# Token-major projections: the gates, branch and output projections of a hybrid block with the weights as the streamed operand

## The chip, the cores and the metric

The kernel is one program on one NeuronCore of one Trainium2 chip. The metric is the device time in microseconds (us) from the first to the last instruction of an execution. The kernel before has a median of 2720.31 us over three runs (2718.95 to 2721.55).

## The reference, cut to what matters

256 tokens of width 2048 pass a mixer (retention and RWKV-7 branches, gated and merged), then an expert layer with 16384 experts. The change touches the second half of the mixer: the two gate projections, the two branch projections, their gated sum, the output projection and the residual.

```python
z = h @ w_in[layer]                       # the last 2*2048 columns of z are the gates
q, k, v, g_ret_out, z_rwkv, gate_ret, gate_rwkv = _split(z, [...])
...
merged = (jax.nn.sigmoid(gate_ret) * (o_ret @ w_ret_branch[layer])
          + jax.nn.sigmoid(gate_rwkv) * (o_rwkv @ w_rwkv_branch[layer]))
x = x + merged @ w_out[layer]
h2 = rms_norm(x, norm2_w[layer])
x = x + peer(h2, ...)
return rms_norm(x, final_norm_w)
```

## The kernel before, in words

Every float32 product is made of three float32r products: both operands are split into a rounded part and a remainder (hi, lo), and hi*hi, hi*lo and lo*hi are added up in PSUM.

**Units and halves.** Weights come in units of 128 partitions x 1024 columns (512 KB). SyncE loads a unit into one of four slots of `raw` (`load_seg`, L280), ScalarE rounds it into `w_hi` in two halves of 512 columns (`hi`, L712; the instruction is L723), VectorE subtracts to get `w_lo` (`lo`, L1071; L1074), and TensorE uses it. `w_hi` and `w_lo` hold two units, so ScalarE may write half n only when half n-4 has been used (`half_used`), and SyncE may load unit n only when unit n-4 has been split (`unit_split`). In the expert layer's first half GpSimd does the subtraction (L1060); in its second half (`vm`, L685) the split is as in the projections.

**Stages.** `SEG` gives for each projection its first unit, its first output group, the groups, the units in a group and the offset in the operand's chunks. In order: `main_rwkv` (52 units), `main_ret` (64), the recurrent part, `gates` (64), `ret` (16), `rwkv` (16), `out` (32), `wq` (32), then the expert layer with 256 units of `peer_u` and 256 of `peer_v`. The stages `gates` to `out` are the 128 units that the change touches.

**A projection** (`project`, L374) keeps the channels of the result on the partitions: a 128x128 block of the weights is the stationary operand and 256 tokens of `act_hi` or `act_lo` (2048 channels on partitions, 256 tokens) stream. A unit takes 24 matmuls of 256 columns, a group is 256 output channels in two PSUM banks of which half is used. The second half of the expert layer (`vm`, L695 to L697) does it the other way: 128 tokens are stationary and 512 weight columns stream, 12 matmuls a unit.

**Between the units** stands other work of the same stages. In `gates` (`head_between`), TensorE does four small sets of matmuls with block-diagonal ones (L593, L599) and a small projection (L606), VectorE one step of the RWKV head norm in each unit from unit 13 (eight reciprocals first, L1327), ScalarE squares and roots. The evacuation of a group stands after the second unit of the next group: sigmoid on ScalarE for `gates` (L803), a product with the gate on VectorE for `ret` (L1359) and `rwkv` (L1362), where the sum of the branches follows (L1364), a copy on ScalarE for `out` (L797). The last group of `gates`, `ret` and `rwkv` is evacuated when TensorE has done the stage; on VectorE the split of the next stage's operand (L1115) or weights comes behind it.

**The end of `out`.** The result has channels on the partitions, so 32 transposes (L618) bring it to tokens on the partitions, VectorE adds x bank by bank (L1373, eight instructions), ScalarE sums the squares (L769, five instructions), and the second norm and its 32 transposes (L416) stand ahead of `wq`. x is loaded again (L320) with the keys behind all loads of `out`.

**PSUM.** Projections use banks 0 to 3, `head_between` uses banks 4 to 7.

## Time and profile before

| | us |
|---|---|
| median of three runs | 2720.31 |
| the profiled execution, whole | 2721.9 |
| its span, first to last instruction | 2720.0 |
| TensorE busy | 2604.2 (96%) |
| VectorE busy | 1738.1 (64%) |
| ScalarE busy | 1259.8 (46%) |
| GpSimd busy | 815.3 (30%) |
| mean granted TensorE clock | 0.988 |

A row of the timeline gives the start and the length of an instruction or of a merged run of them (xcount); the brackets tell how long the engine idled before it and who released it. PE is TensorE, PEld its weight loads, DVE VectorE, ACT ScalarE, SPq the DMA queue of SyncE. Matmuls are pipelined: the length printed of one is longer than the distance to the next, so rates are read from starts. In the rows of stretches each engine has its busy time and, in brackets, its instructions; PEclk is the granted clock as a share of 2.4 GHz.

### The profile page before, as it was taken

Reading aid. Unit: us, or ns where it says so; the run is one execution under the profiler, and the core shown is the slowest. Engines: PE = TensorE matmul, PEld = TensorE weight load, DVE = VectorE, ACT = ScalarE, POOL = GpSimd, SP = SyncE. Lnnn points to the kernel's source line nnn. Section 1 sums busy time; section 2 is a strip of 40 time slices with the busy share of each in tenths; the row PEclk is TensorE's granted clock in tenths of the full one; section 3 lists DMA queues with packets and bytes.
Section 4 is the critical chain, followed back from the end, with each engine's and each line's share of the span. In section 5 each row is a group of like instructions: output and inputs, shape, how many; then the busy total and the mean of one; then the engine's idle time right before and its main releaser. Section 6 shows DMA issues by size and latency. Waiting matters only on the chain.

```text
span 2720.0 us, 57389 instructions
## 1 busy us (share of the span) xinstructions
PE 2604.2 (96%) x18602; PEld 2453.3 (90%) x18602; DVE 1738.1 (64%) x3107; ACT 1259.8 (46%) x2301; POOL 815.3 (30%) x612
## 2 busy tenths in 40 slices
PE   7989988888999999999999999999999999999998
PEld 7989977888999999999999999999988888888876
DVE  4467964333664564558986688778866666666656
ACT  5446532223444444544445543444445555555545
POOL 0021014333000000038988887777730000000000
PEclk9999989999999999999999999999999999999999
DMA  6655530000565556665555555555555565666664
GB/s 203 184 163 163 172 124 1 1 0 0 150 184 163 175 173 180 176 172 178 178 174 173 169 164 158 158 160 157 157 176 192 193 193 193 193 193 192 193 224 162
DMA packets 334661, 429.17 MB, mean 158 GB/s; under 512 B 26885, under 2 KB 299639, under 8 KB 333175
## 3 DMA queue, kind: packets, MB, share of 16 engines
q1 hardware_dynamic: 334583, 428.12, 51.4%
q8 instruction: 50, 0.82, 0.1%
q14 instruction: 28, 0.23, 0.0%
HBM read 423.82 MB, written 4.19 MB: 157 GB/s over the span
## 4 chain that ended last, share of the span: by engine, by line
PE 60%; issue 26%; POOL 10%; DVE 2%; DMA 1%; ACT 1%; POOLq 0%; SPq 0%; DVEq 0%; ACTq 0%
POOL w_lo L1060 9%; PE PS L370 8%; PE PS L371 8%; PE PS L372 8%; PE PS L695 8%; PE PS L696 8%; PE PS L697 8%; PE PS L659 2%; PE PS L534 1%; PE PS L498 1%; PE PS L532 1%; PE PS L523 1%; DVE w_lo L1074 1%; DMA raw<-in_peer_v 0%; PE PS L546 0%
## 5 line engine op out<-in xcount | busy, mean ns | idle before, releaser
L370 PE MATMUL PS<-act_hi,w_hi 128*128 128x256 f32 x4256 | 1218.1, 286 | 30.6 <-DVE w_lo L1074 16.9
L371 PE MATMUL PS<-act_lo,w_hi 128*128 128x256 f32 x4256 | 1207.8, 284 | 0.0
L372 PE MATMUL PS<-act_hi,w_lo 128*128 128x256 f32 x4256 | 1207.6, 284 | 0.0
L1074 DVE TENSOR_TENSOR w_lo<-raw,w_hi 128x512 fp32r<-128x512 f32 x1064 | 720.5, 702 | 308.2 <-ACT w_hi L723 304.9
L1060 POOL TENSOR_TENSOR w_lo<-raw,w_hi 128x512 fp32r<-128x512 f32 x512 | 669.3, 1340 | 675.6 <-ACT w_hi L918 675.6
L370 PEld LDWEIGHTS PS<-act_hi,w_hi 128*128 128x128 f32 x4256 | 819.8, 193 | 37.1 <-issue 19.5
L723 ACT ACTIVATE w_hi<-raw 128x512 fp32r<-128x512 f32 x1064 | 637.7, 624 | 417.0 <-PE PS L372 412.6
L371 PEld LDWEIGHTS PS<-act_lo,w_hi 128*128 128x128 f32 x4256 | 820.1, 193 | 1.0 <-issue 1.0
L372 PEld LDWEIGHTS PS<-act_hi,w_lo 128*128 128x128 f32 x4256 | 819.8, 193 | 0.0
L695 PE MATMUL PS<-w_hi,act_hi 128*128 128x512 f32 x1024 | 399.8, 390 | 3.8 <-DVE w_lo L1074 3.8
L696 PE MATMUL PS<-w_lo,act_hi 128*128 128x512 f32 x1024 | 399.5, 390 | 0.0
L697 PE MATMUL PS<-w_hi,act_lo 128*128 128x512 f32 x1024 | 399.3, 390 | 0.0
L1463 DVE STREAM_TRANSPOSE raw<-raw 128x512 f32<-128x512 f32 x512 | 332.5, 687 | 76.9 <-DMA raw<-in_peer_u 74.6
L918 ACT ACTIVATE w_hi<-raw 128x512 fp32r<-128x512 f32 x512 | 302.9, 627 | 154.3 <-PE PS L372 139.2
L1554 DVE TENSOR_TENSOR act_lo<-big,act_hi 128x256 fp32r<-128x256 f32 x256 | 108.8, 425 | 264.5 <-ACT act_hi L957 258.1
L957 ACT ACTIVATE act_hi<-big 128x256 fp32r (+1 forms) x256 | 106.8, 417 | 321.1 <-PE PS L697 319.7
L695 PEld LDWEIGHTS PS<-w_hi,act_hi 128*128 128x128 f32 x1024 | 192.9, 188 | 44.7 <-DVE w_lo L1074 3.4
L697 PEld LDWEIGHTS PS<-w_hi,act_lo 128*128 128x128 f32 x1024 | 192.9, 188 | 40.3
L696 PEld LDWEIGHTS PS<-w_lo,act_hi 128*128 128x128 f32 x1024 | 192.9, 188 | 39.9
L1471 DVE TENSOR_TENSOR big<-PS,big 128x512 f32 (+1 forms) x64 | 44.2, 691 | 83.1 <-PE PS L659 83.1
L929 ACT ACTIVATE big<-PS 128x256 f32 (+1 forms) x62 | 23.9, 385 | 136.0 <-PE PS L372 136.0
L1489 DVE TENSOR_SCALAR cst<-PS,extra 128x128 f32<-128x128 f32 x256 | 84.8, 393 | 0.0
(243 smaller groups left out, 1684.4 us busy)
## 6 DMA issues: line engine op xcount, KB each, us to landing
raw<-in_peer_u SPq DMA_DIRECT2D x1024, 128.0 KB, 2.7
raw<-in_peer_v SPq DMA_DIRECT2D x256, 512.0 KB, 4.2
raw<-in_w_in SPq DMA_DIRECT2D x180, 512.0 KB, 3.8
raw<-in_w_out SPq DMA_DIRECT2D x32, 512.0 KB, 3.5
raw<-in_peer_w_q SPq DMA_DIRECT2D x128, 128.0 KB, 3.2
raw<-in_w_ret_branch SPq DMA_DIRECT2D x16, 512.0 KB, 3.5
raw<-in_w_rwkv_branch SPq DMA_DIRECT2D x16, 512.0 KB, 3.5
big<-in_x SPq DMA_DIRECT2D x2, 1024.0 KB, 5.9
```

The lines of the kernel that those rows point to most:

```text
L370: pe.matmul(out, wh, xh, start=start, stop=False)
L371: pe.matmul(out, wh, xl, start=False, stop=False)
L372: return pe.matmul(out, wl, xh, start=False, stop=stop)
L695: pe.matmul(out, ah, w_hi[:, k % 2, cols], start=start, stop=False)
L696: pe.matmul(out, ah, w_lo[:, k % 2, cols], start=False, stop=False)
L697: last = pe.matmul(out, al, w_hi[:, k % 2, cols], start=False, stop=stop)
L723: act.activation(w_hi[:, slot % 2, hh * 512:(hh + 1) * 512], raw[:, slot, hh * 512:(hh + 1) * 512], ACT.Copy).then_inc(S["unit_hi"], 1)
L918: act.activation(w_hi[:, k % 2, hh * 512:(hh + 1) * 512].rearrange("p (c s i) -> p c s i", c=4, s=4), u_part(k, 4 * hh, 4), ACT.Copy).then ...
L1060: pool.tensor_tensor(w_lo[:, k % 2, cols].rearrange("p (c s i) -> p c s i", c=4, s=4), u_part(k, 4 * hh, 4), w_hi[:, k % 2, cols].bitcast( ...
L1074: dve.tensor_tensor(w_lo[:, slot % 2, cols], raw[:, slot, cols], w_hi[:, slot % 2, cols].bitcast(f32), ALU.subtract).then_inc(S["unit_spli ...
L1463: dve.transpose(turned, turned).then_inc(S["uT"], 1)
L1554: dve.tensor_tensor(act_lo[:, k % 2, :], g, act_hi[:, k % 2, :].bitcast(f32), ALU.subtract).then_inc(S["act2_split"], 1)
```

## The change

In `gates`, `ret`, `rwkv` and `out` the roles of the operands are exchanged. 128 tokens of `act_hi` or `act_lo` are stationary and 512 weight columns stream; a unit is now 256 input channels x 512 output channels (two chunks), loaded in pieces of 512 columns, and takes 12 matmuls of 512 columns. A group is 512 output channels for all 256 tokens and fills two whole PSUM banks; `gates` has 8 groups of 8 units, `ret` and `rwkv` 4 of 4, `out` 4 of 8. The units of all stages and their number stay.

The results now have tokens on the partitions (`gated`, `merged`). `out` needs its operand with channels on the partitions, so the sum of the branches is transposed, 8 transposes for each 512 channels (`turn_merged`): after units 7, 11 and 15 of `rwkv` and after unit 2 of `out`, into banks 4 to 7. ScalarE and VectorE split the operand straight out of PSUM (`split_act`), for the four parts at units 9 and 13 of `rwkv` and 0 and 4 of `out`. The sum of the branches for a group stands on VectorE in the third unit of the next group (`merge`), for the last group at the end of the stage.

`out` yields x's layout at once: VectorE adds the group in PSUM to x (`evac_out`), ScalarE sums squares in the second unit of a later group (`square_new`), six instead of five instructions. The 32 transposes, the ScalarE copy and the block of eight additions at the end are gone. x and the keys are loaded earlier, behind the loads of the first group of `out` and ahead of the other 24 units' (`load_again`). Evacuations are two instructions of 512 columns for each group of twice the size. `ret`, `rwkv` and `out` are written out in full where they had loops; in `gates` as many units as before are.

```diff
-SEG = {"main_rwkv": (0, 0, 13, 4, 0), "main_ret": (52, 13, 16, 4, 0), "gates": (116, 29, 16, 4, 0), "ret": (180, 45, 8, 2, 0), "rwkv": (196, 53, 8, 2, 8),
-       "out": (212, 61, 8, 4, 0), "wq": (244, 69, 8, 4, 0)}
...

...
-        operand = {"main_rwkv": Z(58, 74), "ret": Z(0, 16), "rwkv": Z(0, 16), "out": Z(58, 74), "wq": Z(16, 32)}
+        def token_loop(eng, name, body):
+            u0, g0, ng, ku, _ = SEG[name]
+            def pair(t):
+                for j in range(2):
...
+            return name in ("ret", "rwkv") and isinstance(g, int) and g == 0 and kq % 2 == 0
+        gated = [flat(Z(82 + 16 * tt, 98 + 16 * tt)) for tt in range(2)]
+        merged = [flat(Z(58 + 8 * tt, 66 + 8 * tt)) for tt in range(2)]
+        def merged_turned(pc):
+            return PS[:, 4 + 2 * (pc % 2):6 + 2 * (pc % 2), :].rearrange("p t (c n) -> p c t n", c=4)
+        def by_chunk(ap):
+            return ap.rearrange("p c (t n) -> p c t n", t=2)
+        operand = {"main_rwkv": None, "ret": Z(0, 16), "rwkv": Z(0, 16), "wq": None}
...
+                def token_body(t, g, base, j):
+                    if name == "out" and g == 1:
+                        load_again()
+                    for kq in range(ku):
+                        slot = kq % 4
+                        sp.wait_ge(S["unit_split"], (base + kq // 4) * 8 + (2 * slot - 6))
+                        sp.dma_start(raw[:, slot, :].rearrange("p (c n) -> p c n", c=2),
+                                     w[:, 2 * kq:2 * kq + 2, ds(g * 512 + col0, 512)]).then_inc(S[f"raw_in{slot}"], 16)
+                if name in BY_TOKEN:
+                    token_loop(sp, name, token_body)
+                    return
...
+            def load_again():
+                sp.wait_ge(S["merged"], 4)
+                sp.dma_start(flat(Z(90, 106)).rearrange("p (a n) -> p a n", a=2),
+                             a["x"][0].rearrange("(a p) n -> p a n", p=P)).then_inc(S["x_again"], 16)
+                sp.dma_start(flat(Z(48, 49))[:, 0:P], a["peer_keys_1"][0]).then_inc(S["keys_in"], 16)
+                sp.dma_start(flat(Z(48, 49))[:, P:2 * P], a["peer_keys_2"][0]).then_inc(S["keys_in"], 16)
...
-            sp.wait_ge(S["merged"], 8)
-            sp.dma_start(flat(Z(90, 106)).rearrange("p (a n) -> p a n", a=2),
-                         a["x"][0].rearrange("(a p) n -> p a n", p=P)).then_inc(S["x_again"], 16)
-            sp.dma_start(flat(Z(48, 49))[:, 0:P], a["peer_keys_1"][0]).then_inc(S["keys_in"], 16)
-            sp.dma_start(flat(Z(48, 49))[:, P:2 * P], a["peer_keys_2"][0]).then_inc(S["keys_in"], 16)
             load_seg("wq", a["peer_w_q"][0], 0)
...
+            def project_tokens(name, between=None):
+                u0, g0, ng, ku, koff = SEG[name]
+                def body(t, g, base, j):
+                    par = (g0 + j) % 2
+                    if name == "out" and g >= 2:
+                        pe.wait_ge(S["x1_done"], 2 * g - 2)
+                    else:
+                        pe.wait_ge(S["proj_evac"], g + (g0 - 1))
+                    for kq in range(ku):
+                        slot, m = kq % 4, base + kq // 4
+                        if name != "gates" and isinstance(g, int) and g == 0 and kq % 2 == 0:
+                            pe.wait_ge(S["act_split"], 4 * nth_operand[name] + (koff + 2 * kq) // 4 + 1)
+                        for hh in range(2):
+                            kc = koff + 2 * kq + hh
+                            cols = slice(hh * 512, (hh + 1) * 512)
+                            first, last_k = kq == 0 and hh == 0, kq == ku - 1 and hh == 1
+                            pe.wait_ge(S["unit_split"], m * 8 + (2 * slot + hh + 1))
+                            for tt in range(2):
+                                out = PS[:, 2 * par + tt, :]
+                                ah, al = act_hi[:, kc, tt * P:(tt + 1) * P], act_lo[:, kc, tt * P:(tt + 1) * P]
+                                pe.matmul(out, ah, w_hi[:, slot % 2, cols], start=first, stop=False)
+                                pe.matmul(out, ah, w_lo[:, slot % 2, cols], start=False, stop=False)
+                                last = pe.matmul(out, al, w_hi[:, slot % 2, cols], start=False, stop=last_k)
+                            last.then_inc(S["half_used"], 1)
+                        if between and isinstance(g, int):
+                            between(g * ku + kq)
+                token_loop(pe, name, body)
...
                     last.then_inc(S["gate_up"], 1)
-            project("gates", head_between)
-            project("ret")
-            project("rwkv")
-            project("out")
-            pe.wait_ge(S["proj_evac"], 69)
-            for gi in range(8):
-                tt, cg = gi // 4, gi % 4
-                for c in range(4):
-                    last = pe.transpose(PS[:, gi, c * P:(c + 1) * P], big[:, 4 * cg + c, tt * P:(tt + 1) * P], ident)
-                last.then_inc(S["dT_done"], 1)
+            project_tokens("gates", head_between)
+            project_tokens("ret")
+            def turn_merged(pc):
+                pe.wait_ge(S["merged"], pc + 1)
+                if pc >= 2:
+                    pe.wait_ge(S["act_split"], 4 * nth_operand["out"] + pc - 1)
+                for tt in range(2):
+                    for c in range(4):
+                        last = pe.transpose(PS[:, 4 + 2 * (pc % 2) + tt, c * P:(c + 1) * P],
+                                            merged[tt][:, (4 * pc + c) * P:(4 * pc + c + 1) * P], ident)
+                last.then_inc(S["merged_T"], 1)
+            def rwkv_turns(unit):
+                if unit in (7, 11, 15):
+                    turn_merged(unit // 4 - 1)
+            def out_turns(unit):
+                if unit == 2:
+                    turn_merged(3)
+            project_tokens("rwkv", rwkv_turns)
+            project_tokens("out", out_turns)
             pe.wait_ge(S["keys_in"], 32)
             pe.wait_ge(S["x1_done"], 8)
             for w in range(2):
...
+                def body(t, g, base, j):
+                    for kq in range(ku):
...
+                        for hh in range(2):
+                            hi(base + kq // 4, kq % 4, hh)
+                        if kq == 1 and evac and not (isinstance(g, int) and g == 0):
+                            act.wait_ge(S["half_used"], base * 8)
+                            evac(g - 1, (g0 + j + 1) % 2)
+                        if between and isinstance(g, int):
+                            between(g * ku + kq)
+                token_loop(act, name, body)
+                if evac:
+                    act.wait_ge(S["half_used"], 2 * (u0 + ng * ku))
+                    evac(ng - 1, (g0 + ng - 1) % 2)
             def split_act(name, kq):
                 pc = SEG[name][4] // 4 + kq
...
+                    return
                 if name in ("main_rwkv", "wq"):
                     act.wait_ge(S["xT_done" if name == "main_rwkv" else "x2T_done"], pc + 1)
                     for kc in range(4 * pc, 4 * pc + 4):
...
@@ -798,11 +898,11 @@
                                    PS[:, 2 * par:2 * par + 2, 0:TOK], ACT.Copy).then_inc(S["proj_evac"], 1)
                 return evac
-            def evac_sigmoid(base):
-                def evac(g, par):
-                    act.activation(big[:, ds(g * 2 + base, 2), :] if not isinstance(g, int) else big[:, base + 2 * g:base + 2 * g + 2, :],
-                                   PS[:, 2 * par:2 * par + 2, 0:TOK], ACT.Sigmoid).then_inc(S["proj_evac"], 1)
-                return evac
+            def evac_sigmoid(g, par):
+                for tt in range(2):
+                    dst = gated[tt][:, g * 512:(g + 1) * 512] if isinstance(g, int) else gated[tt][:, ds(g * 512, 512)]
+                    last = act.activation(dst, PS[:, 2 * par + tt, :], ACT.Sigmoid)
+                last.then_inc(S["proj_evac"], 1)
             split_seg("main_rwkv", evac_copy(32))
...
@@ -893,14 +993,25 @@
                 if 0 <= q < 2:
...
-            split_seg("gates", evac_sigmoid(82), head_between)
+            split_tokens("gates", evac_sigmoid, head_between)
             sqrt_table()
-            split_seg("ret")
-            split_seg("rwkv")
-            split_seg("out", evac_copy(0))
-            for tt, k, at, end in ((0, 0, 0, 2), (0, 1, 2, 4), (1, 0, 0, 2), (1, 1, 2, 3), (1, 2, 3, 4)):
-                act.wait_ge(S["x1_done"], 4 * tt + end)
-                square(xs[tt][:, 512 * at:512 * end], xn[tt][:, 512 * at:512 * end], tt, k)
+            split_tokens("ret")
+            def rwkv_turned(unit):
+                if unit in (9, 13):
+                    split_act("out", unit // 4 - 2)
+            def out_turned(unit):
+                if unit in (0, 4):
+                    split_act("out", 2 + unit // 4)
+            def square_new(g, par):
+                k, at = max(0, g - 1), 0 if g == 1 else 512 * g
+                for tt in range(2 if g > 0 else 0):
+                    act.wait_ge(S["x1_done"], 2 * g + tt + 1)
+                    square(xs[tt][:, at:512 * g + 512], xn[tt][:, at:512 * g + 512], tt, k)
+            split_tokens("rwkv", None, rwkv_turned)
+            split_tokens("out", square_new, out_turned)
             act.wait_ge(S["kT_done"], 1)
             act.activation(keysT, PS[:, 7, 0:256], ACT.Copy).then_inc(S["keysT"], 1)
             norm(xs, xn, 1)
...
@@ -1348,29 +1484,47 @@
                 for start, steps in stages:
                     if unit >= start:
                         next(steps, None)
...
-            def chunks2(g, base):
-                return big[:, base + 2 * g:base + 2 * g + 2, :] if isinstance(g, int) else big[:, ds(g * 2 + base, 2), :]
             def evac_ret(g, par):
-                dve.tensor_tensor(chunks2(g, 82), PS[:, 2 * par:2 * par + 2, 0:TOK], chunks2(g, 82), ALU.mult).then_inc(S["proj_evac"], 1)
+                for tt in range(2):
+                    cols = gated[tt][:, g * 512:(g + 1) * 512]
+                    last = dve.tensor_tensor(cols, PS[:, 2 * par + tt, :], cols, ALU.mult)
+                last.then_inc(S["proj_evac"], 1)
             def evac_rwkv(g, par):
-                dve.tensor_tensor(chunks2(g, 98), PS[:, 2 * par:2 * par + 2, 0:TOK], chunks2(g, 98), ALU.mult).then_inc(S["proj_evac"], 1)
+                for tt in range(2):
+                    cols = gated[tt][:, 2048 + g * 512:2048 + (g + 1) * 512]
+                    last = dve.tensor_tensor(cols, PS[:, 2 * par + tt, :], cols, ALU.mult)
+                last.then_inc(S["proj_evac"], 1)
...
+            def merge(g):
                 dve.wait_ge(S["proj_evac"], g + (SEG["rwkv"][1] + 1))
-                dve.tensor_tensor(chunks2(g, 58), chunks2(g, 82), chunks2(g, 98), ALU.add).then_inc(S["merged"], 1)
-            dve.wait_ge(S["proj_evac"], 45)
-            split_seg("ret", evac_ret)
-            split_seg("rwkv", evac_rwkv)
-            split_seg("out")
-            dve.wait_ge(S["x_again"], 16)
...
-                dve.wait_ge(S["dT_done"], gi + 1)
-                cols = slice(gi * 512, (gi + 1) * 512)
-                dve.tensor_tensor(flat(Z(90, 106))[:, cols], flat(Z(90, 106))[:, cols], PS[:, gi, :], ALU.add).then_inc(S["x1_done"], 1)
+                for tt in range(2):
+                    last = dve.tensor_tensor(merged[tt][:, g * 512:(g + 1) * 512], gated[tt][:, g * 512:(g + 1) * 512],
+                                             gated[tt][:, 2048 + g * 512:2048 + (g + 1) * 512], ALU.add)
+                last.then_inc(S["merged"], 1)
...
+                    split_act("out", 2 + unit // 4)
+            def evac_out(g, par):
+                if g == 0:
+                    dve.wait_ge(S["x_again"], 16)
+                for tt in range(2):
+                    x1 = flat(Z(90 + 8 * tt, 98 + 8 * tt))[:, g * 512:(g + 1) * 512]
+                    dve.tensor_tensor(x1, x1, PS[:, 2 * par + tt, :], ALU.add).then_inc(S["x1_done"], 1)
```

In ScalarE's and VectorE's `split_act` for `out`, ScalarE waits for `merged_T` and copies `merged_turned(pc)` from PSUM to `act_hi`, and VectorE subtracts it from the same place into `act_lo`. VectorE's `split_tokens` mirrors ScalarE's, with `later(g - 1)` at the third unit of a group and `later(ng - 1)` at the end.

## Rows read from the trace of the kernel before

**Rows 1.** First part of the page: busy time, share, instructions.
```profile
PE 2604.2 (96%) x18602; PEld 2453.3 (90%) x18602; DVE 1738.1 (64%) x3107; ACT 1259.8 (46%) x2301; POOL 815.3 (30%) x612
```
**Rows 2.** Stretches: gates, out, and most of the expert layer's second half.
```profile
681.50:876.50 195.00, 195.00 (x1570) 190.43 (x1568) 115.44 (x154) 92.54 (x146) 0.00 (x0) 1.00 0.60 173
...
981.70:1075.60 93.90, 93.86 (x768) 93.68 (x768) 45.46 (x65) 42.24 (x68) 0.00 (x0) 0.98 0.66 200
...
2003.00:2600.00 597.00, 596.11 (x2640) 493.68 (x2639) 372.95 (x659) 321.53 (x662) 0.23 (x1) 1.00 0.60 192
```
**Rows 3.** Timeline of PE in out, first and last of 28 matmuls.
```profile
1059.72 0.28 PE L371 MATMUL PS<-act_lo,w_hi 128*128 128x256 f32 x1
...
1062.96 0.28 PE L371 MATMUL PS<-act_lo,w_hi 128*128 128x256 f32 x1
```
**Rows 4.** Timeline of PE in the expert layer's second half, first and last of 16.
```profile
2299.65 0.39 PE L696 MATMUL PS<-w_lo,act_hi 128*128 128x512 f32 x1
...
2303.05 0.39 PE L696 MATMUL PS<-w_lo,act_hi 128*128 128x512 f32 x1
```
**Rows 5.** Timeline of DVE in gates, two of the eight reciprocal steps.
```profile
727.84 1.74 DVE L1327 RECIPROCAL big<-big 128x256 f32<-128x256 f32 x1
729.62 1.29 DVE L1074 TENSOR_TENSOR w_lo<-raw,w_hi 128x512 fp32r<-128x512 f32 x2
730.83 1.75 DVE L1327 RECIPROCAL big<-big 128x256 f32<-128x256 f32 x1
```
**Rows 6.** Timelines of ACT, DVE and PE where one stage follows another.
```profile
876.67 0.60 ACT L803 ACTIVATE big<-PS 128x512 f32<-128x512 f32 x1 [5.12 <-PE PS L372]
...
930.66 0.69 DVE L1359 TENSOR_TENSOR big<-PS,big 128x512 f32<-128x512 f32 x1 [3.80 <-PE PS L372]
931.27 1.21 DVE L1115 TENSOR_TENSOR act_lo<-big,act_hi 128x1024 fp32r<-128x1024 f32 x1
...
933.23 0.36 PE L370 MATMUL PS<-act_hi,w_hi 128*128 128x256 f32 x1 [2.61 <-DVE w_lo L1074]
...
979.58 0.69 DVE L1362 TENSOR_TENSOR big<-PS,big 128x512 f32<-128x512 f32 x1
980.30 0.69 DVE L1364 TENSOR_TENSOR big<-big 128x512 f32<-128x512 f32 x1
```
**Rows 7.** Timelines of PE, DVE and ACT from out's last matmul to the norm.
```profile
1075.32 0.28 PE L372 MATMUL PS<-act_hi,w_lo 128*128 128x256 f32 x1
1076.29 3.71 PE L618 MATMUL PS<-cst,big 128*128 128x128 f32 x32 [0.69 <-ACT big L797]
...
1083.16 0.16 DVE L1120 TENSOR_REDUCE small<-small 128x2 f32<-128x6 f32 x1 [1.25 <-ACT big L769]
...
1082.43 0.61 ACT L769 ACTIVATE big<-big 128x512 f32<-128x512 f32 x1
```
**Rows 8.** Stretches around the four changes of stage, for the granted clock (PEclk).
```profile
880.50:887.50 7.00, 5.70 (x27) 5.73 (x28) 4.79 (x7) 3.08 (x6) 0.00 (x0) 0.51 0.46 139
...
930.00:933.00 3.00, 0.63 (x6) 0.42 (x4) 2.34 (x3) 0.63 (x1) 0.00 (x0) 1.00 0.00 0
...
983.00:986.50 3.50, 3.50 (x19) 3.50 (x18) 2.14 (x3) 0.98 (x2) 0.00 (x0) 0.51 0.77 227
...
1082.00:1089.00 7.00, 4.41 (x20) 4.07 (x21) 3.38 (x8) 6.47 (x15) 0.00 (x0) 0.51 0.00 0
```
**Rows 9.** Expert layer, second half: timelines of SP, ACT and PE; last the DMA issues' view.
```profile
2602.59 0.38 SPq L352 DMA_DIRECT2D big<-x_scratch  x1
2603.03 0.46 SPq L354 DMA_DIRECT2D big<-in_final_norm_w  x1
...
2617.32 1.15 ACT L723 ACTIVATE w_hi<-raw 128x512 fp32r<-128x512 f32 x2 [3.71 <-DMA raw<-in_peer_v]
...
2618.73 0.80 PE L695 MATMUL PS<-w_hi,act_hi 128*128 128x512 f32 x1 [2.94 <-DVE w_lo L1074]
...
big<-in_x SPq DMA_DIRECT2D x1, 2048.0 KB, 8.3
```

More of the change, by code:

```diff
@@ L31 @@
 NVEC = VROWS + 16
-SEG = {"main_rwkv": (0, 0, 13, 4, 0), "main_ret": (52, 13, 16, 4, 0), "gates": (116, 29, 16, 4, 0), "ret": (180, 45, 8, 2, 0), "rwkv": (196, 53, 8, 2, 8),
-       "out": (212, 61, 8, 4, 0), "wq": (244, 69, 8, 4, 0)}
+SEG = {"main_rwkv": (0, 0, 13, 4, 0), "main_ret": (52, 13, 16, 4, 0), "gates": (116, 29, 8, 8, 0), "ret": (180, 37, 4, 4, 0), "rwkv": (196, 41, 4, 4, 8),
+       "out": (212, 45, 4, 8, 0), "wq": (244, 45, 8, 4, 0)}
+BY_TOKEN = ("gates", "ret", "rwkv", "out")
 U0, V0 = 276, 532
@@ L43 @@
 LANDED["v"] = LANDED["u"] + 64 * (BLOCKS // 2)
-PEEL = {"main_ret": 8, "gates": 4}
+PEEL = {"main_ret": 8, "gates": 2, "ret": 2, "rwkv": 2, "out": 2}
 PREP_MIX, PREP_LORA_IN, PREP_LORA_W, PREP_DECAY, PREP_EXP, PREP_LORA_A, PREP_A = 3, 12, 14, 16, 20, 21, 23
@@ L761, in split_act @@
                     act.wait_ge(S["orwkv"], 2)
-                if name == "out":
-                    act.wait_ge(S["merged"], 2 * pc + 2)
-                    act.wait_ge(S["half_used"], 2 * SEG["rwkv" if pc < 2 else "out"][0])
                 act.activation(act_hi[:, 4 * pc:4 * pc + 4, :], operand[name][:, 4 * pc:4 * pc + 4, :], ACT.Copy).then_inc(S["act_hi"], 1)
@@ L1083, in body @@
                         ahead = name in ("main_rwkv", "wq") and kq == 0
-                        if name in operand and isinstance(g, int) and g == 0 and not (name == "out" and kq < 2) and not ahead:
+                        if name in operand and isinstance(g, int) and g == 0 and not ahead:
                             split_act(name, kq)
@@ L1095, in split_seg @@
                 seg_loop(dve, name, body, PEEL[name] if between else 1)
-                if name == "rwkv":
-                    split_act("out", 0)
-                    split_act("out", 1)
                 if evac:
@@ L1374, in _ @@
+            split_tokens("ret", evac_ret)
+            split_tokens("rwkv", evac_rwkv, rwkv_turned, merge)
+            split_tokens("out", evac_out, out_turned)
             norm(1, x_tok, xn_tok)
```

49 lines of the change are left out of this document (45 added, 4 removed).

## The prediction, made before the changed kernel was run

> **What bounds the kernel now.** I read the page first: TensorE is busy 96% of the span, VectorE 64%, ScalarE 46% [rows 1]. So time can come only from TensorE's own pace or from the places where it stands still. The view by stretches then shows that this holds in the stages of the change: in `gates` TensorE is busy 195.00 of 195.00 us with 0.60 of the DMA engines' time used, in `out` 93.86 of 93.90 us [rows 2]. A busy share is no pace, so the next view is the timeline of TensorE, read from start to start. In `out` 27 distances take 1062.96 - 1059.72 = 3.24 us, 0.120 us for a matmul of 256 columns [rows 3]. In the expert layer's second half, which already has tokens stationary and 512 weight columns streaming, 15 distances take 2303.05 - 2299.65 = 3.40 us, 0.2267 us for 512 columns [rows 4]. Streaming alone takes 256/2.4 = 107 ns and 512/2.4 = 213 ns at the full clock, so either width carries about 13 ns more for each matmul. A unit costs 24 x 0.120 = 2.88 us now, and 12 x 0.2267 = 2.72 us in the new form. That is the heart of the change. All else is edges: three changes of stage, the end of `out`, and whether the other engines and the loads keep up with 2.72 us.
>
> **The changed stream.** 64 + 16 + 16 + 32 = 128 units x 0.16 us = **-20.5 us**, all on the path. The nearest row is very near: the same shapes, the same split engines, 512 KB for each unit. That stretch holds its pace for 597 us at 192 GB/s with the DMA engines 0.60 used [rows 2], so the loads are no new bound; the pieces of 2 KB (they were 1 KB) lie between the 1 KB of `out`, which ran at 200 GB/s [rows 2], and the 4 KB of the expert layer. Bounds for this term: 0 (the 13 ns are not for each matmul, see the rivals) and -20.5.
>
> **VectorE in `gates`.** The tightest unit holds a reciprocal and two subtractions, 730.83 - 727.84 = 2.99 us from one to the next [rows 5], above 2.72. It happens eight times, units 13 to 20. VectorE may run ahead of TensorE by three halves, 4.08 us, of which rounding and subtracting a half take 0.6 + 0.7 (1.15 and 1.29 for two [rows 5, 9]); 2.7 us are left. A reciprocal in front of a half delays it by 1.75 + 0.65 - 1.36 = 1.05 us, and each unit adds 0.27. TensorE's own insertion after unit 15 (the small projection) gives it time, and the five units behind it reach 1.05 + 4 x 0.27 = 2.1 us. So I take 0, with 2 us as the other bound if that cover fails. ScalarE's crowded place is unit 9, with two sigmoids, two table switches and a root, 4.8 us in a row; behind it stands TensorE's set of matmuls with ones (some 3.4 us), which covers it. Those sets are the same as before.
>
> **The changes of stage.** At the end of `gates` ScalarE evacuates, switches its table and rounds the next operand while TensorE waits: a second sigmoid of 0.60 us stands in this chain now, and the last matmul lasts 0.11 us longer (0.39 for 0.28) [rows 3, 4, 6]: +0.7. At the end of `ret` VectorE evacuates (0.69), splits the operand (1.21) and the first weights, and TensorE stood 2.61 us [rows 6]; a second evacuation goes in: +0.8. At the end of `rwkv` evacuation and sum (0.69 + 0.69, [rows 6]) become four instructions: 2 x 0.69 + 0.11 = +1.5. Queued behind them on VectorE are the first subtraction of `out` and the third part of the operand's split; TensorE is the one who waits. Together **+3.0 us**.
>
> **The transposes.** 32 of them took 3.71 us [rows 7], so 8 take 0.93, and with the late first matmul behind them I take 1.05 for a set (bounds 0.9 and 1.6, the latter if TensorE drains on either side). Four sets: the one after unit 15 of `rwkv` lies in the wait just counted, three are on the path: **+3.2 us**. What each waits for is ready: the sum of group g is done in the third unit of group g+1 and the transposes stand after the fourth. VectorE has in `rwkv` at unit 9 an evacuation (1.38) and a part of the operand's split (1.21), 2.6 us, just under the 2.7 us of its lead, then the sum; I take 0, with 1 us as a bound.
>
> **Sums of squares in `out`.** In unit 17 ScalarE waits for VectorE's additions and then does two squares of 1024 columns, some 3.8 us between two roundings where 4.08 - 0.6 is free: +0.3.
>
> **The end of `out`.** From the start of the last matmul to the reduction that opens the norm now 1083.16 - 1075.32 = 7.84 us pass [rows 7]: a copy, the transposes, eight additions in a row, squares. In the new kernel: 0.43 until the matmul is done, an addition of 0.69, then the second addition beside the first square; the second square starts at about 1.85 and takes 0.61 and a short read of the sum: 2.65 us. **-5.2 us**. What is late next is the same norm and the same 32 transposes as before, with nothing new in front.
>
> **The earlier load of x.** 2 MB and the keys now go out when unit 3 of `out` has been split, ahead of unit 8's weights on SyncE. There is an event like it: 3 MB went out at 2602.59 and 2603.03 amid the streaming of the second half; the next unit's weights were late, ScalarE waited 3.71 us for them until 2617.32 and TensorE stood 2.94 us [rows 9]. So about 11 us of lead were there and 14.7 were needed for 3 MB. 2 MB landed in 8.3 us at the end of `out` [rows 9]; with the unit behind them I get 11 to 12 us. The lead here has one set of transposes more in it, 12 us. I take 0; the other bound is what the 3 MB did, 3 us and a stretch of low clock. VectorE needs x itself only in unit 9, some 16 us after the issue, and is covered.
>
> **The clock.** It fell to half (0.51 where 1.00 is 2.4 GHz) for 7.0 us after the wait at the end of `gates`, for 3.5 us after the one at the end of `rwkv`, not after the 2.61 us at the end of `ret`, and for 7.0 us at the end of `out` [rows 8]. A low stretch costs half its length when TensorE streams. The waits at `ret` and `rwkv` become 0.8 and 1.5 us longer, so a new stretch of 3.5 us is possible at each, 1.7 us of loss; at the end of `out` TensorE now stands still for less. I take +1.0, bounds -2 and +3.5.
>
> **Sum.** -20.5 + 3.0 + 3.2 + 0.3 - 5.2 + 1.0 = -18.2 us. The profiled execution has a span of 2720.0 us in 2721.9; it is 1.6 us above the median of 2720.31. The new span is 2701.8, and against the median 2720.3 - 18.2 = **2702 us**.
>
> **A page beside it.** The Trainium skill, "TensorE: Matmul & The Clock Gate", section "Back-to-back issue gap", gives N/2.4 plus about 2.5 ns for a single matmul at the full clock, 109 ns at 256 columns and 216 ns at 512. The rows show 120 and 227, so the trace doesn't agree; by that rule the new width would bring an estimated 12 x 2.5 ns a unit, 3.8 us in 128 units instead of 20.5, and the time would be 2719, beside the partial form of rival D. The measurement of both widths in this kernel decides for me.
>
> **The rivals.** *A: the forecast*, 0.72.
>
> *B: the load of x starves the stream.* For it: the row of 3.71 us. Against it: a third fewer bytes, and a set of transposes inside the lead. Price 2.94 us and a low stretch of 7 us, half lost: 6.4 us, 2708. Chance 0.16.
>
> *C: VectorE or ScalarE becomes the bound* in the crowded units (13 to 20 of `gates`, 9 of `rwkv`, 17 of `out`). For it: 2.99 against 2.72, and 2.6 of lead 2.7. Price at most 8 x 0.27 + 1 + 1 = 4 us, 2706. Chance 0.06.
>
> *D: the width brings little.* The 13 ns would then be no fixed share of a matmul but of what surrounds it in a projection (operands, evacuations), and a 512-column matmul would take 0.24 there. Then only the edges are left: +3.0 + 3.2 + 0.3 + 1.0 - 5.2 = +2.3, 2722.6. Against it: rows 4. A part of it, say 15 us of the 20.5 lost, gives 2717 and is no change either. Chance 0.04 for the two.
>
> *E, slower: the clock.* If longer waits and transposes between the stages brought TensorE down and it stayed low through a stage instead of 3.5 or 7 us, each unit would lose its streaming time once more, 12 x 0.213 = 2.6 us. From 18.2 / 2.6 = 7 units on it eats the whole gain; 16 units, the whole of `ret`, cost 41 us and give 2743. For it: three of four edges had a low stretch. Against it: none outlasted 7 us [rows 8], and the form itself ran 597 us at 1.00 [rows 2]. Chance 0.02.
>
> **How the numbers follow.** The likeliest is A, 2702. Its own bounds: 2696.5 (no loss to the clock and 2 us back, sets of 0.9 us, less at the end) to 2706 (sets of 1.6, 3.5 us of clock). Reaching to B and C takes the upper end to 2709. D and E stay outside, 0.06, and some of B. A measurement of this kernel can tell about 0.2%, 5.4 us, from no change. Faster: A, B and C, 0.94. No change: D, 0.04. Slower: E, 0.02.
>
> **What would show it.** Starts 0.227 us apart and 2.72 us from unit to unit in all four stages; 1.05 us for each set of transposes; waits of about 6, 3.5 and 3.9 us (the last with a set in it) between the stages; 2.65 us from the last matmul of `out` to the norm's reduction. B would show as a wait of ScalarE for weights of unit 8 or 9 of `out`, C as TensorE waiting for `w_lo` inside a stage, D as 0.24 us from start to start, E in the granted clock of a whole stage. The prediction is wrong if a stage's pace is above 2.75 us a unit.

## The result, and the profile after

The changed kernel takes 2704.25 us (median of 4 runs, 2702.05 to 2706.31) against 2720.93 of the kernel before: a ratio of 0.9942, 95% interval 0.9926 to 0.9958. The forecast was 2702, 18.2 us less than before; 16.7 us less were measured. The interval of the ratio reaches from 11 to 20 us less, so the times alone can't tell 18.2 from 16.7. The profiled execution is the slowest of the four; it has a span of 2704.5 us, 15.5 less than before.

The stretches of the changed kernel, cut at the same events as in [rows 2] (length, then busy time and instructions of PE, PEld, DVE, ACT, POOL, then the granted clock, the DMA engines' share and GB/s); the stages `gates`, `ret`, `rwkv`, `out`, and the way from `out` to `wq`:

```profile
681.90:866.70 184.80, 184.80 (x802) 150.19 (x800) 115.24 (x154) 91.94 (x145) 0.00 (x0) 1.00 0.62 182
872.60:918.60 46.00, 46.00 (x192) 37.75 (x192) 25.49 (x38) 21.39 (x34) 0.00 (x0) 0.94 0.56 183
922.10:969.10 47.00, 47.00 (x208) 38.84 (x209) 31.06 (x46) 21.02 (x32) 0.00 (x0) 0.96 0.56 179
972.70:1062.70 90.00, 89.87 (x392) 73.87 (x392) 48.41 (x71) 41.62 (x69) 0.00 (x0) 0.98 0.65 211
1062.70:1073.20 10.50, 6.64 (x37) 6.21 (x35) 6.83 (x15) 8.89 (x20) 0.00 (x0) 0.67 0.17 41
```

`gates` fell from 195.0 to 184.8 us with the same work of the other engines in it, and TensorE is still busy all the time. `rwkv` gained nothing: it now holds two sets of transposes and a low stretch of the clock. Inside the stream the timeline of TensorE in `out` reads, first and last of 17 matmuls:

```profile
1039.67 0.39 PE L461 MATMUL PS<-w_hi,act_hi 128*128 128x512 f32 x1
...
1043.30 0.39 PE L462 MATMUL PS<-w_lo,act_hi 128*128 128x512 f32 x1
```

16 distances take 3.63 us, 0.2269 each, as in [rows 4]; a unit is 2.72 us. The edges, from the timelines of PE, of DVE and of PE around one set of transposes:

```profile
872.60 0.77 PE L461 MATMUL PS<-w_hi,act_hi 128*128 128x512 f32 x1 [5.66 <-DVE w_lo L1185]
922.08 0.64 PE L461 MATMUL PS<-w_hi,act_hi 128*128 128x512 f32 x1 [3.21 <-DVE w_lo L1185]
972.68 0.47 PE L461 MATMUL PS<-w_hi,act_hi 128*128 128x512 f32 x1 [2.53 <-DVE w_lo L1185]
...
969.32 1.29 DVE L1500 TENSOR_TENSOR big<-PS,big 128x512 f32<-128x512 f32 x2 [4.09 <-PE PS L463]
970.64 1.29 DVE L1506 TENSOR_TENSOR big<-big 128x512 f32<-128x512 f32 x2
...
945.54 1.03 PE L685 MATMUL PS<-cst,big 128*128 128x128 f32 x8
946.33 0.48 PE L461 MATMUL PS<-w_hi,act_hi 128*128 128x512 f32 x1
946.64 0.40 PE L462 MATMUL PS<-w_lo,act_hi 128*128 128x512 f32 x1
```

The doubled evacuation and sum at the end of `rwkv` stand there as two pairs where [rows 6] has two single ones. A set of transposes takes 0.79 us, and the next matmul is 0.08 late: 0.87. At the end of `out` [rows 7] are answered by

```profile
1062.57 0.39 PE L463 MATMUL PS<-w_hi,act_lo 128*128 128x512 f32 x1
...
1062.99 1.28 DVE L1523 TENSOR_TENSOR big<-big,PS 128x512 f32<-128x512 f32 x2 [4.08 <-PE PS L463]
1065.14 0.16 DVE L1256 TENSOR_REDUCE small<-small 128x2 f32<-128x6 f32 x1 [0.87 <-ACT big L869]
```

1065.14 - 1062.57 = 2.57 us from the last matmul to the norm, for 7.84. The low stretches of the clock (PEclk 0.5, that is 1.2 GHz, where 1.00 is 2.4 GHz), to be held against [rows 8]: the ends of `gates`, `ret` and `rwkv`, then one in the expert layer, whose code is the same in both kernels:

```profile
870.90:877.70 6.80, 5.10 (x12) 4.11 (x13) 5.19 (x7) 3.28 (x6) 0.00 (x0) 0.51 0.40 139
922.10:925.50 3.40, 3.40 (x8) 2.63 (x9) 2.77 (x4) 0.55 (x1) 0.00 (x0) 0.52 0.42 153
973.30:976.70 3.40, 3.40 (x10) 2.67 (x9) 2.87 (x4) 0.63 (x1) 0.00 (x0) 0.52 0.43 157
...
1406.80:1410.20 3.40, 3.02 (x14) 3.02 (x15) 3.37 (x5) 1.22 (x2) 3.40 (x4) 0.52 0.15 38
```

**Where the 15.5 us came from.** Read from first and last starts of matmuls: `gates` -10.2, `ret` -2.7, `rwkv` +0.8, `out` -3.7, the three edges +0.6, +0.7 and +1.3, from the last matmul of `out` to the first of `wq` -4.7 (10.61 for 15.26). That makes -17.9. The work ahead of `gates` came out 0.4 longer and the part behind it 1.9 longer (1631.3 us from `wq` on for 1629.4), both without a change in the code. Of the 1.9, 0.9 is a longer wait behind the burst of [rows 9] (3.81 us for 2.94). The low stretch at 1406.8 cost 0.7: from its first matmul to the next pause of TensorE above 1.2 us 68.81 us pass (1407.18 to 1475.99), in the kernel before 68.12 (1424.33 to 1492.45). That is less than half of its 3.4 us. The likely reason, not tested, is that TensorE doesn't set the pace there: GpSimd (POOL) is busy for all of the 3.40 us in that row, TensorE for 3.02.

### The profile page after: what moved, and what is told of

Its sections match the earlier page's. It is cut to its first block, busy times and chain, and to the rows that moved or that the text cites. A ratio compares the mean times of both kernels' runs of the same rounds, so it can differ in the third digit from the quotient of the medians.

```text
span 2704.5 us, 53711 instructions
## 1 busy us (share of the span) xinstructions
PE 2587.5 (96%) x17066; PEld 2374.2 (88%) x17066; DVE 1735.4 (64%) x3107; ACT 1255.1 (46%) x2295; POOL 814.9 (30%) x612
## 4 chain that ended last, share of the span: by engine, by line
PE 61%; issue 25%; POOL 10%; DVE 2%; DMA 1%; ACT 1%; POOLq 0%; SPq 0%; DVEq 0%; ACTq 0%
POOL w_lo L1171 9%; PE PS L407 9%; PE PS L408 9%; PE PS L409 9%; PE PS L774 8%; PE PS L776 8%; PE PS L775 8%; PE PS L738 2%; PE PS L601 1%; PE PS L565 1%; PE PS L599 1%; PE PS L590 1%; DVE w_lo L1185 1%; DMA raw<-in_peer_v 0%; PE PS L613 0%
## 5 line engine op out<-in xcount | busy, mean ns | idle before, releaser
L407 PE MATMUL PS<-act_hi,w_hi 128*128 128x256 f32 x3232 | 925.3, 286 | 20.2 <-POOL w_lo L1171 12.7
L408 PE MATMUL PS<-act_lo,w_hi 128*128 128x256 f32 x3232 | 916.8, 284 | 0.0
L409 PE MATMUL PS<-act_hi,w_lo 128*128 128x256 f32 x3232 | 916.7, 284 | 0.0
L407 PEld LDWEIGHTS PS<-act_hi,w_hi 128*128 128x128 f32 x3232 | 622.4, 193 | 25.5 <-POOL w_lo L1171 12.8
L408 PEld LDWEIGHTS PS<-act_lo,w_hi 128*128 128x128 f32 x3232 | 622.7, 193 | 0.2 <-issue 0.2
L409 PEld LDWEIGHTS PS<-act_hi,w_lo 128*128 128x128 f32 x3232 | 622.4, 193 | 0.0
L774 PE MATMUL PS<-w_hi,act_hi 128*128 128x512 f32 x1024 | 399.6, 390 | 4.7 <-DVE w_lo L1185 4.7
L775 PE MATMUL PS<-w_lo,act_hi 128*128 128x512 f32 x1024 | 399.3, 390 | 0.0
L776 PE MATMUL PS<-w_hi,act_lo 128*128 128x512 f32 x1024 | 399.2, 390 | 0.0
L461 PE MATMUL PS<-w_hi,act_hi 128*128 128x512 f32 x512 | 203.7, 398 | 11.5 <-DVE w_lo L1185 11.4
L462 PE MATMUL PS<-w_lo,act_hi 128*128 128x512 f32 x512 | 201.6, 394 | 0.0
L463 PE MATMUL PS<-w_hi,act_lo 128*128 128x512 f32 x512 | 201.3, 393 | 0.0
```

The source lines that it names most:

```text
L407: pe.matmul(out, wh, xh, start=start, stop=False)
L408: pe.matmul(out, wh, xl, start=False, stop=False)
L409: return pe.matmul(out, wl, xh, start=False, stop=stop)
L461: pe.matmul(out, ah, w_hi[:, slot % 2, cols], start=first, stop=False)
L774: pe.matmul(out, ah, w_hi[:, k % 2, cols], start=start, stop=False)
L775: pe.matmul(out, ah, w_lo[:, k % 2, cols], start=False, stop=False)
```

## The experiments

**The control, and the width alone.** The first of them is the changed kernel again.

> The changed kernel once more, with nothing altered, as the control of this group. 2704 us (0.994 of the kernel before). Two readings of its trace matter. First, whether the three low stretches of the clock after the waits at the ends of gates, ret and rwkv (6.8, 3.4 and 3.4 us in the first trace) come back at the same places: if the waits cause them, they do. Second, the low stretch after a wait of 2.49 us in the untouched expert layer (at 1407 us): there the kernel before had the same wait of 2.49 us and no low stretch, so I expect it to be chance, present or absent here with nothing else changed, worth 1.7 us.

Measured: 2700.96 us, ratio 0.993 (0.9911 to 0.9949). The three low stretches at the edges came back with the same lengths. So did the one in the expert layer, behind the same wait, and at the same price of 0.7 us, not the 1.7 that I had expected:

```profile
1406.17 0.58 PE L407 MATMUL PS<-act_hi,w_hi 128*128 128x256 f32 x1 [2.49 <-POOL w_lo L1171]
```

The kernel before waits 2.49 us at the same point and keeps its clock; the kernel with filled waits (below) does too. Both profiles of one kernel agree, which speaks against my expectation that it is drawn anew in each execution. That it goes with where in time the wait falls is a reading that nothing here tests. The last low stretch in mid-stream, behind the 3 MB burst of [rows 9], is missing in the control: there TensorE waited 0.69 us, in the first profile of the same kernel 3.81. The spans of that kernel are 2704.5 and 2698.0, 6.5 apart: 3.1 of this wait, 2.6 of the low clock behind it (5.2 us of matmuls at half the clock), and 0.8 ahead of `gates`.

> Undoes the width alone: tokens stay stationary, all else stays as in the changed kernel, but each matmul of 512 weight columns becomes two of 256 (only the opening matmuls of a group stay 512 wide). Theory 'about 13 ns for each matmul, whatever its width': starts 0.120 us apart, 2.88 us a unit, and 128 x 0.16 x 0.93 = 19 us back: 2723 us, 1.001 of the kernel before. Rival 'the faster pace comes with the layout (pieces of 2 KB, whole banks, tokens stationary) and not with the width': the unit stays at 2.72 us and the time at 2704, 0.994.

```diff
-                                pe.matmul(out, ah, w_hi[:, slot % 2, cols], start=first, stop=False)
-                                pe.matmul(out, ah, w_lo[:, slot % 2, cols], start=False, stop=False)
-                                last = pe.matmul(out, al, w_hi[:, slot % 2, cols], start=False, stop=last_k)
+                                nn = 512 if first else 256
+                                for w0 in range(0, 512, nn):
+                                    part_ = slice(hh * 512 + w0, hh * 512 + w0 + nn)
+                                    o = out[:, w0:w0 + nn]
...
```

Measured: 2720.5 us, ratio 1.0001 (0.9991 to 1.0011), 19.5 us above the control (19 expected). In `gates` two of its matmuls stand 12 distances apart (769.95 and 771.39, 0.120 each):

```profile
769.95 0.28 PE L467 MATMUL PS<-w_hi,act_lo 128*128 128x256 f32 x1
771.39 0.28 PE L467 MATMUL PS<-w_hi,act_lo 128*128 128x256 f32 x1
```

By the times the width alone carries the gain; everything else of the change, edges and tail together, comes out at nothing. Rival D falls. The trace adds something that the times hide. The waits at the ends of `ret` and `rwkv` are as long as in the control (3.21 and 2.53 us), but no low stretch follows:

```profile
933.61 0.47 PE L465 MATMUL PS<-w_hi,act_hi 128*128 128x512 f32 x1 [3.21 <-DVE w_lo L1189]
984.79 0.47 PE L465 MATMUL PS<-w_hi,act_hi 128*128 128x512 f32 x1 [2.53 <-DVE w_lo L1189]
...
933.60:937.00 3.40, 3.40 (x23) 3.15 (x24) 3.40 (x5) 0.95 (x2) 0.00 (x0) 1.00 0.45 133
984.80:988.20 3.40, 3.40 (x23) 3.14 (x24) 3.38 (x5) 0.94 (x2) 0.00 (x0) 1.00 0.43 139
```

From the first matmul of `gates` to the last of `out` 396.2 us pass (681.48 to 1077.67), in the control 380.5 (681.07 to 1061.53): 15.7 more, and 19.1 once the two missing stretches (1.7 us each) are put back. Behind these stages the burst took about as much again in this execution (a wait of 2.64 us for 0.69, and a low stretch of 3.4 us). So the 19 of the theory stand, but that the two times differ by just that is partly luck. Each of these matmuls has a weight load of its own ([rows 2]: 1570 and 1568), so the run tells the number of pairs and not whether the 13 ns belong to the matmul or to its load. The Trainium skill, "TensorE: Matmul & The Clock Gate", section "Back-to-back issue gap", would have given an estimated 3.5 us for this undoing (2.5 ns for each of the matmuls more); the measurement decides.

> The width once more, in the ret stage alone (16 units): each matmul of 512 columns there becomes four of 128, but for the opening ones of a group. Theory '13 ns for each matmul': 53 + 13 = 67 ns from start to start, 48 a unit, 3.2 us a unit, ret some 7 us longer. Rival 'at this width the loading of the stationary operand sets the pace': 0.107 us or so, as for the transposes of 128 columns, 5.1 us a unit, ret some 33 us longer.

The diff is the one above with 128 in `ret` and 512 elsewhere. One execution, 2759.87 us: 56 to 59 us above the changed kernel, far beyond either theory. Stretches and two pairs of starts in `ret`:

```profile
870.00:914.20 44.20, 42.44 (x187) 41.31 (x188) 11.67 (x17) 8.38 (x14) 0.00 (x0) 0.50 0.21 68
914.40:928.00 13.60, 13.60 (x125) 13.60 (x123) 3.16 (x6) 3.15 (x5) 0.00 (x0) 1.00 0.25 85
930.00:970.00 40.00, 40.00 (x348) 39.50 (x348) 11.90 (x18) 10.86 (x17) 0.00 (x0) 1.00 0.34 103
...
899.95 0.41 PE L465 MATMUL PS<-w_hi,act_hi 128*128 128x128 f32 x1
901.87 0.41 PE L465 MATMUL PS<-w_hi,act_hi 128*128 128x128 f32 x1
...
910.19 0.73 PE L465 MATMUL PS<-w_hi,act_hi 128*128 128x512 f32 x1
912.43 0.63 PE L467 MATMUL PS<-w_hi,act_lo 128*128 128x512 f32 x1
...
942.76 0.27 PE L466 MATMUL PS<-w_lo,act_hi 128*128 128x128 f32 x1
945.89 0.27 PE L467 MATMUL PS<-w_hi,act_lo 128*128 128x128 f32 x1
```

Two things at once. At the full clock 28 distances take 3.13 us, 0.112 each, nearly what 256 columns cost: so a matmul of 128 columns isn't 53 + 13 ns, and "13 ns for each matmul whatever its width" holds from 256 to 512 columns and not below. The pace is near the 0.107 of the rival; that the loading of the stationary operand sets it was not tested. And TensorE, busy without a pause from 871.8 us on, stayed at the low clock (9 distances in 1.92 us, 0.213) until 914.2 us, a stretch of 44 us counted from inside the wait. The 512-column stream left it after 6.8 us, counted in the same way. Just before the clock rose TensorE had run the six opening matmuls of the second group, the first with 512 columns since the stage's own opening (910.19 to 912.43); behind them it ran the narrow ones at the full clock. Whether the wide ones brought it back was not tested.

> The kernel without waits at the edges (e_edges), and in ret alone each matmul of 512 columns becomes four of 128. In e_128ret, where TensorE came into ret from a wait of 5.7 us, the clock was low for 44 us of unbroken matmuls of 128 columns, and these stood 0.213 us apart, at the full clock 0.111. Question: is it the narrow matmuls that keep the clock low, or what came before? Theory 'narrow matmuls don't raise a low clock, but leave a high one alone': no low stretch in ret here, 48 x 0.111 = 5.35 us a unit, ret 42 us longer than in e_edges, about 2725 us. Rival 'at this width the clock is low in any case': it falls without a wait before it, and ret takes up to 10 us a unit, 2760 us or more.

Measured: one execution, 2719.53 us, 35 above the kernel without waits at the edges; its `ret` runs at the full clock from end to end:

```profile
865.00:940.00 75.00, 75.00 (x645) 73.82 (x644) 26.15 (x39) 22.45 (x36) 0.00 (x0) 1.00 0.36 113
```

14 of the 16 units are narrow, 14 x (5.35 - 2.72) = 37 us. So the narrow matmuls don't bring the clock down. Behind a wait that had brought it down they ran on without its coming back.

**The clock at the edges.**

> Changes nothing of the waits between the stages, but fills them on TensorE with matmuls on constants into banks that nobody reads: five of 512 columns in float32 at the end of gates, three at the end of ret, two at the end of rwkv (about 0.76 us each). Theory 'each of the three low stretches of the clock comes from TensorE standing still there': they vanish, 3.4 + 1.7 + 1.7 us are gained less up to 1 us for first matmuls that start late: about 2698 us, 0.992. Rival 'the low stretches come in any case and the filling is only more work': 2704 or up to 2 us more, 0.994 to 0.995.

```diff
             project_tokens("gates", head_between)
+            pe.wait_ge(S["orwkv"], 2)
+            fill(5)
             project_tokens("ret")
+            fill(3)
...
             project_tokens("rwkv", rwkv_turns)
+            fill2(2)
```

`fill` and `fill2` are matmuls of the identity with 512 columns of constants in float32; their results are not used. Measured: 2699.33 us, ratio 0.991 (0.9891 to 0.9929), against 0.993 of the control. By the medians that is 1.6 us less than the control, and the intervals overlap, so the times don't show a gain. The traces do. All three stretches are at the full clock, and TensorE is idle for 1.4, 0.6 and 0.8 us in these rows:

```profile
870.00:877.00 7.00, 5.63 (x23) 3.93 (x22) 6.06 (x8) 4.76 (x9) 0.00 (x0) 1.00 0.38 122
917.00:923.00 6.00, 5.37 (x20) 3.49 (x19) 5.91 (x9) 2.01 (x3) 0.00 (x0) 1.00 0.30 89
966.00:972.00 6.00, 5.19 (x19) 3.32 (x19) 5.88 (x9) 3.13 (x5) 0.00 (x0) 1.00 0.28 83
```

From the first matmul of `ret` to the last of `out` 184.3 us pass (872.50 to 1056.79), in the control 189.8 (871.78 to 1061.53): 5.5 less. The three stretches account for 5.9: 1.7 us of the first lie inside the wait of the changed kernel, so it costs half of 5.1 and not of 6.8, and the other two cost 1.7 each. The time shows little of it because the burst of [rows 9] made TensorE wait 3.87 us in this execution, with a low stretch behind it, and 0.69 us in the control, without one.

**The edges themselves.**

> The same at one edge alone, the end of ret: its last evacuation on VectorE moves into the second unit of rwkv. The wait of 3.2 us and the low stretch of 3.4 us behind it (1.7 us lost) go and the rest stays: 4.9 us less than the changed kernel, about 2698 us. If the low stretch belonged to something else, it stays and 3.2 us are gained.

```diff
-            split_tokens("ret", evac_ret)
-            split_tokens("rwkv", evac_rwkv, rwkv_turned, merge)
+            split_tokens("ret", evac_ret, carry=True)
+            split_tokens("rwkv", evac_rwkv, rwkv_turned, merge, prev=evac_ret)
```

Measured: 2694.7 us, ratio 0.991 (0.9891 to 0.993). Wait and low stretch at the end of `ret` are gone; the wait of 2.53 us at the end of `rwkv` is still there, this time without a low stretch. Against the control's 0.993 it is some 5 us, near the 4.9 expected, with overlapping intervals. In the trace it is more: from the first matmul of `ret` to the last of `out` 183.2 us (870.98 to 1054.14) for 189.8. Of the 6.6 us 3.2 are the wait, 1.7 the clock behind it, and 1.7 the stretch at `rwkv` that nothing in this edit took away; the agreement of the median is partly luck.

> Takes away what the three changes of stage wait for: the last group of gates, ret and rwkv is evacuated (and the last sum made) in the second and third unit of the next stage, as inside a stage, since the next stage's first group uses the other banks; the operand of ret is split without waiting for the end of gates. Nothing is left out. Theory 'the edges are waits in TensorE's path, and each brings a low stretch of the clock': the waits of 5.7, 3.2 and 2.5 us and the stretches of 6.8, 3.4 and 3.4 us (half of it lost) go, 11.4 + 6.8 = 18 us less up to 1 us for crowded units: about 2684 us, 0.987. Rival 'the waits only move: VectorE and ScalarE are late in the first units of the next stage instead': TensorE waits there for w_lo, and half of it or less is gained, 0.990 or more.

```diff
+                        if kq == 1 and prev and isinstance(g, int) and g == 0:
+                            dve.wait_ge(S["half_used"], base * 8)
+                            prev(3, (g0 + 1) % 2)
+                        if kq == 2 and prev_later and isinstance(g, int) and g == 0:
+                            prev_later(3)
...
-            dve.wait_ge(S["proj_evac"], SEG["ret"][1])
...
+            split_tokens("rwkv", evac_rwkv, rwkv_turned, merge, prev=evac_ret, carry=True)
+            split_tokens("out", evac_out, out_turned, prev=evac_rwkv, prev_later=merge)
```

ScalarE has the same for the last sigmoid, its switch of tables stands behind `ret`, the second part of the operand of `ret` is split one unit earlier, and the third part of the operand of `out` one unit later. Measured: 2684.65 us, ratio 0.9867 (0.985 to 0.9884), 2684 and 0.987 expected. TensorE has no wait from `gates` to the last matmul of `out`; around the former first edge:

```profile
850.00:880.00 30.00, 30.00 (x134) 24.87 (x133) 18.19 (x26) 16.53 (x27) 0.00 (x0) 1.00 0.63 194
```

The waits did not move elsewhere. From the first matmul of `gates` to the last of `out` 362.9 us pass (681.20 to 1044.05), 17.6 less than in the control; the waits (11.4) and the clock behind them (5.9) make 17.3.

**The bursts of loads.**

> Doubles the suspected cost of the earlier load: a second 2 MB (a copy that nothing uses) is loaded beside x ahead of unit 8 of the output projection. Theory 'the earlier load costs nothing because the lead of some 12 us covers 2 MB but not 4': ScalarE waits for the weights of unit 8 some 3 to 6 us, TensorE 2 to 5 us, with a low stretch of the clock behind it; 2706 to 2711 us. Rival 'the units' loads overtake it, bytes don't matter': no wait in out and 2702 us.

```diff
+                sp.dma_start(flat(Z(106, 122)).rearrange("p (a n) -> p a n", a=2),
+                             a["x"][0].rearrange("(a p) n -> p a n", p=P)).then_inc(S["x_more"], 16)
...
+                if g == 1:
+                    act.wait_ge(S["x_more"], 16)
```

One execution, 2705.66 us (2706 to 2711 expected). In the changed kernel ScalarE waited a little for a unit behind x, and TensorE did not; with twice the bytes both did, and the clock fell for 3.4 us (first row: changed kernel; the others: 4 MB, ACT and PE):

```profile
994.01 1.19 ACT L802 ACTIVATE w_hi<-raw 128x512 fp32r<-128x512 f32 x2 [1.53 <-DMA raw<-in_w_out]
```
```profile
997.46 1.15 ACT L804 ACTIVATE w_hi<-raw 128x512 fp32r<-128x512 f32 x2 [6.52 <-DMA raw<-in_w_out]
998.96 0.74 PE L463 MATMUL PS<-w_hi,act_hi 128*128 128x512 f32 x1 [3.25 <-DVE w_lo L1189]
```

So 2 MB just fit into the lead and the term of 0 holds, with under 2 us to spare: of the wait of 6.52 us on ScalarE 3.25 reached TensorE, so 3.27 were covered, and x itself uses 1.53 of them.

> The three edges as in the first kernel of this group, and the 3 MB that the end of the expert layer needs (x again and the last norm's weights) loaded in 24 pieces of 128 KB between the units instead of in one burst. In the traces so far that burst makes TensorE wait 0 to 4.5 us and sometimes brings a low stretch of 6.8 us, so executions of one kernel differ by up to 6 us. Theory: both go: 3 to 6 us less than with the edges alone, about 2680 us, 0.985, with a smaller spread. Rival 'the bytes cost the same in pieces': as the edges alone, 0.987.

```diff
+                            if n % 2 == 0:
+                                q = n // 2
+                                tt, part_ = q // 8, slice((q % 8) * 256, (q % 8 + 1) * 256)
+                                sp.dma_start(flat(Z(8 * tt, 8 * tt + 8))[:, part_], x1_dram[tt * P:(tt + 1) * P, part_]).then_inc(S["x1_in"], 16)
+                            elif n % 4 == 1:
+                                part_ = slice((n // 4) * 256, (n // 4 + 1) * 256)
+                                sp.dma_start(flat(Z(16, 24))[:, part_], fw[:, part_]).then_inc(S["fw_in"], 16)
```

Measured: 2680.7 us (four runs from 2680.45 to 2681.4), ratio 0.9853 (0.9837 to 0.987). TensorE doesn't wait in that stretch any more, where it waited 3.93 us in the profile with the edges alone. The intervals of the two ratios overlap, but all four runs are faster than the fastest with the edges alone (2683.51), and they lie within 1 us where those lie within 4.6:

```profile
2560.00:2600.00 40.00, 40.00 (x178) 33.13 (x177) 25.26 (x45) 21.20 (x44) 0.00 (x0) 1.00 0.75 230
```

This is the fastest version: by the ratios 40 us under the kernel before and 21 to 24 under the changed one (0.993 and 0.9942).

## Why the prediction was right, step by step

The mechanism held: a shorter stream, against it edges and transposes that cost about what was said. In the stages of the change the forecast was off by 0.4 us (-17.8 from the unrounded starts for -18.2). The other 2.3 us that the two spans differ from it lie in code that the change doesn't touch, for which the forecast had no term.

**The stream** (-20.5): right, and the term that carries the result. The starts in both traces show 0.120 and 0.227, and undoing the width alone gave back 19.5 us in the times and 19.1 by the traces. The reason given for it was too wide: the 13 ns are no constant of a matmul, as the width of 128 shows.

**VectorE in `gates`** (0): right. Reciprocals still follow each other at 2.99 us in the trace after (726.34, 729.33), and TensorE shows no wait there.

**The edges** (+0.7, +0.8, +1.5): measured +0.6, +0.7, +1.3 from start to start.

**The transposes** (+3.2 for three sets): 0.87 for a set and not 1.05, so +2.6. The term was a little too large.

**Squares in `out`** (+0.3): right. ScalarE was held up in unit 17, and one matmul behind it started 0.3 late (a distance of 0.52 at 1024.58).

**The end of `out`** (-5.2): -5.3 to the norm's reduction (2.57 for 7.84). Of it 4.7 arrive at `wq`: the norm's transposes ran on the low clock for longer, 5.96 us to the first matmul of `wq` for 5.34.

**The clock** (+1.0): a little small. A new stretch of 3.4 us at the end of `ret`, the chance the forecast named, is 1.7 us. Those at `gates` and `rwkv` stayed, the first with 5.1 us of matmuls in it for 5.7 before, 0.3 less: together about +1.4. One in untouched code came with it, another 0.7, which no step of the forecast looked at.

**The load of x** (0, with rival B): no wait of TensorE in `out`. It was closer than 0 sounds: ScalarE waited 1.53 us, and the 4 MB run shows the cliff and its price, a wait of 3.25 us and a low stretch.

Rival C did not show, D fell to the 256-column run, E did not show in the changed kernel. A relative of E showed itself in an experiment, with narrow matmuls behind a wait. "None outlasted 7 us" was true of the four changes of stage in [rows 8] only: elsewhere in the kernel before, where TensorE is busy for only 4.68 of 13.70 us, the clock was low for all of that time.

```profile
382.30:396.00 13.70, 4.68 (x11) 3.82 (x12) 11.20 (x7) 0.13 (x1) 7.80 (x3) 0.50 0.01 2
```

## What to carry to other kernels

When an engine is busy all the time, read its pace from starts, and look for a stage of the same kernel that does the same work in another shape: it priced this change to 1 us in 20. The waits where one stage follows another were not part of the change's idea, yet evacuating the last group inside the next stage gained as much again (about 16 us), because the waits were paid a second time in clock: 11.4 us of wait and 5.9 of clock. A burst of bytes ahead of a stream was free up to the stream's lead (2 MB) and cost wait and clock beyond it (4 MB, one execution); 3 MB in pieces between the units made TensorE wait nowhere in that stage. And spans of two profiles differ by what a burst does in each, so compare an experiment stage by stage, from start to start.

## What the runs showed of the hardware that I had not expected

- float32r matmuls of 128, 256 and 512 columns with a new stationary operand each time start 0.112, 0.120 and 0.227 us apart at the full clock. At the low clock 512 columns take 0.427 (874.01 and 874.44 in the changed kernel), 256 take 0.213 (882.79 and 883.01 in the kernel before) and 128 take 0.213 as well. The Trainium skill, "TensorE: Matmul & The Clock Gate", section "Back-to-back issue gap", gives N/1.2 ns there; that agrees at 512 and 256 and not at 128.
- A TensorE that had waited 5.7 us stayed at 1.2 GHz for 44 us while 128-column matmuls ran without a gap, and for 6.8 us with 512 columns. The same narrow stream without the wait ran at 2.4 GHz throughout. Both narrow runs are single executions.
- Waits of 2.5 to 3.2 us sometimes bring a low stretch of 3.4 us and sometimes none, behind the same wait: at the end of `rwkv` (2.53 us) yes in the changed kernel and no in the one with one edge moved and in the one with 256 columns, at the end of `ret` (3.21 us) yes in the changed kernel and no with 256 columns. What decides it was not tested.
- A low stretch doesn't always cost half its length: in the part of the expert layer where GpSimd is busy throughout, 3.4 us of low clock cost 0.7 (both profiles of the changed kernel).
